# GpSimd's first operation on each weight chunk: a one-source multiply and add in place of the addition of a zero column

## The chip, the cores and the metric

The kernel runs on one core of a Trainium2 chip. The metric is the device time of one launch in microseconds. The notes below call the engines PE (TensorE), DVE (VectorE), ACT (ScalarE), POOL (GpSimd) and SP (SyncE), as the profile does.

## The reference, cut to what matters

A diffusion backbone of four layers takes 512 latent tokens and 128 context tokens (640 columns in all) of width 1024 through one step. Each layer is a token mixer and a dense SwiGLU network:

```
for layer in range(4):
    mixer = (latent attention, bidirectional RWKV-7, multi-scale pooling, latent attention)[layer]
    y = layer_norm(ALPHA * y + gate1 * mixer(modulate(y)))
    y = layer_norm(ALPHA * y + gate2 * swiglu(modulate(y)))      # 1024 -> 2816 -> 1024
```

All arrays are float32. Nearly all of the arithmetic is `h @ W` with a weight matrix that is used once.

## The kernel before

**Split products.** PE multiplies in a rounded float32 type (fp32r). To keep the precision, both factors are split: `hi` is the value rounded to fp32r, `lo` is the value minus `hi`. Each product is the sum of three passes, `w_hi * h_hi + w_lo * h_hi + w_hi * h_lo`. The activations stand as 8 tiles of 128 x 640 (features on partitions, tokens on columns). A matmul takes one 128 x 128 weight tile and 320 columns, so a weight tile costs six matmuls.

**The weight stream.** All weights lie in HBM as 354 chunks of 8 tiles (128 x 1024 elements), in the order of use. SP loads chunk after chunk into `w_raw`, a ring of RAW = 3 slots. POOL turns each into `w_hi` (L680) and `w_lo` (L682) in rings of RS = 4 slots, in the function `split`. POOL may write slot n % 4 once PE has begun with chunk n - 3 (semaphore `w_used`), and PE may read chunk n once `w_split` has counted n + 1. SP loads a new chunk once `w_split` has passed the chunk that stood in its slot. POOL also does small work of the attention heads (`m_diag` L802, `m_hlo` L796) and of the RWKV heads (L712 to L786, among them `s_ys` L763). Its function `stream` walks over the chunks; where 24 chunks or more lie ahead it does so in a hardware loop whose body is 12 chunks, with waits on values that are worked out from the loop's register.

**The activations' side.** At the start of each product stage ACT writes the hi part of each of the 8 tiles, and DVE the lo part as a subtraction of two SBUF tensors: `f_hlo` and `m_hlo` (L2382), in the opening of the RWKV layer `r_hlo` (L2550). There DVE also makes `r_t` (L2566), the token shift with its six mixing weights: 48 tiles of `r_t` and 48 of `r_hlo`. PE's panels (L857, L907) wait for the lo parts tile by tile. In the first attention layer DVE multiplies `x` by a constant (L2279, 8 tiles in place) before the attention output is added to it. In the pooling layer DVE makes the window sums `p_b` (L2854).

**Beside the feed-forward panels.** In layers 0 to 2 DVE also works out the next layer's modulation (`f_acc` L2264, L2262) from SBUF tensors, eight instructions for each of the 22 feature tiles; within one such tile of 128 features PE uses two chunks. DVE also makes `f_a` (L2407) and its lo part `f_alo` (L2409) there.

The order on each engine is that of the code; engines meet only at semaphores.

Of the kernel before, what the change touches and what calls it, by code (L numbers as in the profile page):

```python
# [19 lines left out]
ALU = mybir.AluOpType  # L20
# [3 lines left out]
P = 128  # L24
# [22 lines left out]
CH = 8  # L47
RAW, RS = 3, 4
# [174 lines left out]
def build(nc, a, o):  # L223
    ctx = ExitStack()
    with ctx:
        def sb(name, shape, dt=F32, st=None):
            return (st or ctx).enter_context(nc.sbuf_tensor(name, shape, dt))

        def sem(name):
            return ctx.enter_context(nc.semaphore(name))  # L230
# [4 lines left out]

        x = sb("x", [P, KD, T])
        raw = sb("w_raw", [P, RAW, CH * P])
        zrow = sb("zrow", [P, 1])
        cst = sb("cst", [P, NCST])
        mods = [sb(f"mod{i}", [P, 48, 2]) for i in range(2)]  # L240
        eps = sb("eps", [P, 5])
# [28 lines left out]
        w_hi_done = sem("w_hi_done")  # L270
# [4 lines left out]
        s_init, s_const, s_x = sem("s_init"), sem("s_const"), sem("s_x")  # L275
# [146 lines left out]
        whi = sb("w_hi", [P, RS, CH * P], F32R)  # L422
# [246 lines left out]

        @block.gpsimd  # L670
        def _(pool):
            nc.gpsimd.memset(zrow[:, :], 0.0).then_inc(s_init, 1)
            pool.wait_ge(s_init, 1)

            def split(raw_slot, slot, land, used, n1):
                pool.wait_ge(w_land[raw_slot], land)
                if used is not None:

                    pool.wait_ge(w_used, used)
                nc.gpsimd.tensor_tensor(whi[:, slot, :], raw[:, raw_slot, :], zrow[:, 0:1].to_broadcast([P, CH * P]), ALU.add).then_inc(w_hi_done, 1)  # L680
                pool.wait_ge(w_hi_done, n1)
                nc.gpsimd.tensor_tensor(wlo[:, slot, :], raw[:, raw_slot, :], whi[:, slot, :].bitcast(F32),  # L682
                                        ALU.subtract).then_inc(w_split, 1)

            body = RAW * RS

            def stream(first, last):
                n = first
                while n < last:
                    if n >= body and n % body == 0 and last - n >= 2 * body:  # L690
                        with pool.Fori(n // body, last // body) as i:
                            for u in range(body):
                                split(u % RAW, u % RS, i * (16 * RS) + 16 * (u // RAW + 1), i * body + (u - RS + 1), i * body + (u + 1))
                        n = last // body * body
                    else:
                        split(n % RAW, n % RS, 16 * (n // RAW + 1), n - RS + 1 if n >= RS else None, n + 1)
                        n += 1

            def heads():
                m, q = m_rwb, q_rwb  # L700
# [67 lines left out]
                for i in spans():  # L768
# [11 lines left out]
                    if 0 <= i - 1 < FINAL:  # L780
                        normed(i - 1)
                stream(heads_at, heads_at + 2)
                pool.wait_ge(q.y, 10 * PAIRS)
                pool.wait_ge(q.emptied, FILL["bonus", FINAL])
# [4 lines left out]
            def attention(L):  # L789
                m, q = m_mla[L], q_mla[L]  # L790
                chunk = LAYER_BASE[L] + HEADS_AT + HEADS_AHEAD

                def lo_part(j):
                    for n, (t0, t1) in enumerate(((0, TS), (TS, T))):
                        pool.wait_ge(q.ohi, q.at.ohi + 2 * j + n + 1)
                        nc.gpsimd.tensor_tensor(m.hlo[:, j, t0:t1], m.O[:, t0:t1], m.hhi[:, j, t0:t1].bitcast(F32), ALU.subtract).then_inc(q.olo, 1)  # L796

                def diagonal(j, u):
                    pool.wait_ge(q.rec, q.at.rec + 5 * j + u // 2 + 1)
                    if j:  # L800
                        pool.wait_ge(q.av, q.at.av + 5 * j - (1 if u < 8 else 0))
                    nc.gpsimd.tensor_tensor(m.diag[:, u, :], ident, m.rc[:, u:u + 1].to_broadcast([P, P]), ALU.mult).then_inc(q.diag, 1)  # L802

                for j in range(HEADS // 2):
                    if j:
                        lo_part(j - 1)
                    stream(chunk + j, chunk + j + 1)
                    for u in range(BLOCKS):
                        diagonal(j, u)
                lo_part(HEADS // 2 - 1)  # L810

            mixed = MIXER.index(1)
            heads_at = LAYER_BASE[mixed] + C_RWKV_LORA + C_RWKV_UP + C_RWKV_RKV
            stream(0, HEADS_AT + HEADS_AHEAD)
            attention(0)
            stream(HEADS_AT + HEADS_AHEAD + HEADS // 2, LAYER_BASE[mixed])
            landed, order = [0] * RAW, rwkv_chunks()

            def rwkv_pieces(n0, n1):

                for n, runs in enumerate(order[n0:n1], LAYER_BASE[mixed] + n0):
                    if len(runs) > 1:
                        landed[n % RAW] += 16 * (len(runs) - 1)
                        pool.wait_ge(w_part[n % RAW], landed[n % RAW])
                    split(n % RAW, n % RS, 16 * (n // RAW + 1), n - RS + 1, n + 1)
# [765 lines left out]
        def _(act):  # L1591
# [601 lines left out]


            act.wait_ge(s_const, 16)
            act.wait_ge(s_init, 2)
            ch(af(sc_c[:, :, :], cond, ACT.Silu))
            nc.scalar.copy(sc_hi[:, :, :], sc_c[:, :, :]).then_inc(s_init, 1)
            end()
# [12 lines left out]
        def _(dve):  # L2212
# [682 lines left out]
            nc.vector.memset(eps[:, 2:3], GN_EPS)  # L2895
            nc.vector.memset(eps[:, 3:5], 0.0).then_inc(s_init, 1)
            dve.wait_ge(s_const, 16)
            dve.wait_ge(s_init, 3)
            ch(tt(sc_lo[:, :, :], sc_c[:, :, :], sc_hi[:, :, :].bitcast(F32), ALU.subtract))
            ch(tt(fold, ident[0:4, 0:2], ident[0:4, 2:4], ALU.add))  # L2900
            end()
# [202 lines left out]
```

## Time and profile before

| | us |
|---|---|
| median of 3 runs | 3827.82 |
| lowest and highest of them | 3827.03, 3828.3 |
| span of the profiled execution, first to last instruction | 3817.3 |
| PE busy | 3511.2 |
| DVE busy | 2410.5 |
| POOL busy | 1930.7 |
| ACT busy | 963.8 |

The profiled execution has no time of its own beside its span; the median of the runs stands 10.5 us above that span, which is the work around the first and the last instruction. The busy times overlap: they say how long each engine worked, not what the others waited for.

### The profile page before, as it was taken

Reading aid. Unit: us, or ns where it says so; the run is one execution under the profiler, and the core shown is the slowest. Engines: PE = TensorE matmul, PEld = TensorE weight load, DVE = VectorE, ACT = ScalarE, POOL = GpSimd, SP = SyncE. Lnnn points to the kernel's source line nnn. Section 1 sums busy time; section 2 is a strip of 40 time slices with the busy share of each in tenths; the row PEclk is TensorE's granted clock in tenths of the full one; section 3 lists DMA queues with packets and bytes.
Section 4 is the critical chain, followed back from the end, with each engine's and each line's share of the span. In section 5 each row is a group of like instructions: output and inputs, shape, how many; then the busy total and the mean of one; then the engine's idle time right before and its main releaser. Section 6 shows DMA issues by size and latency. Waiting matters only on the chain.

```text
span 3817.3 us, 74078 instructions
## 1 busy us (share of the span) xinstructions
PE 3511.2 (92%) x31676; PEld 3294.7 (86%) x31676; DVE 2410.5 (63%) x3150; ACT 963.8 (25%) x1950; POOL 1930.7 (51%) x1067
## 2 busy tenths in 40 slices
PE   6899999999789788889999995899999999999998
PEld 2777899999788678888999995799999777899997
DVE  6355688667884467746784769886576555622125
ACT  5433230001243345542300013300012433310010
POOL 1333556665265646626566552466564333566662
PEclk9999999999899889999999997899999999999999
DMA  8200134333145534332343431244332100122221
GB/s 326 62 18 18 45 105 147 129 112 116 67 149 179 147 82 103 87 95 66 123 143 116 127 100 46 90 138 139 112 115 74 31 18 18 56 78 78 73 77 50
DMA packets 226857, 367.67 MB, mean 96 GB/s; under 512 B 104753, under 2 KB 111089, under 8 KB 226417
## 3 DMA queue, kind: packets, MB, share of 16 engines
q1 hardware_dynamic: 171408, 255.08, 22.1%
q10 hardware_dynamic: 55136, 107.98, 8.2%
q8 instruction: 250, 4.10, 0.4%
q14 instruction: 63, 0.51, 0.0%
HBM read 326.47 MB, written 36.54 MB: 95 GB/s over the span
## 4 chain that ended last, share of the span: by engine, by line
PE 77%; DVE 13%; ACT 2%; issue 2%; DMA 2%; SPq 1%; POOL 0%; ACTq 0%; DVEq 0%; POOLq 0%
PE ps L857 58%; PE ps L1118 3%; PE ps L907 2%; PE ps L1131 2%; PE ps L1149 2%; DVE r_t L2566 1%; PE ps L924 1%; DVE x L2362 1%; DVE r_hlo L2550 1%; PE ps L1090 1%; PE ps L1072 1%; DVE x L2371 1%; DVE ps L2715 1%; DVE m_mx L2494 1%; DVE s_T L2714 1%
## 5 line engine op out<-in xcount | busy, mean ns | idle before, releaser
L680 POOL TENSOR_TENSOR w_hi<-w_raw,zrow 128x1024 fp32r<-128x1024 f32 x354 | 695.3, 1964 | 1225.5 <-PE ps L857 879.1
L682 POOL TENSOR_TENSOR w_lo<-w_raw,w_hi 128x1024 fp32r<-128x1024 f32 x354 | 900.3, 2543 | 27.7
L2264 DVE SCALAR_TENSOR_TENSOR f_acc<-f_unit,silu_c,f_acc 128x512 f32<-128x512 f32 x504 | 630.8, 1292 | 7.6
L857 PE MATMUL ps<-f_hhi,w_hi 128*128 128x320 f32 x2688 | 634.2, 317 | 0.0
L857 PE MATMUL ps<-f_hhi,w_lo 128*128 128x320 f32 x2688 | 613.0, 309 | 0.0
L857 PE MATMUL ps<-f_hlo,w_hi 128*128 128x320 f32 x2688 | 610.7, 308 | 0.0
L857 PEld LDWEIGHTS ps<-f_hlo,w_hi 128*128 128x128 f32 x2688 | 449.6, 188 | 0.0
L857 PEld LDWEIGHTS ps<-f_hhi,w_lo 128*128 128x128 f32 x2688 | 449.0, 188 | 0.0
L857 PEld LDWEIGHTS ps<-f_hhi,w_hi 128*128 128x128 f32 x2688 | 441.1, 188 | 0.0
L857 PE MATMUL ps<-f_ahi,w_hi 128*128 128x320 f32 x1408 | 322.0, 310 | 0.0
L857 PE MATMUL ps<-f_alo,w_hi 128*128 128x320 f32 x1408 | 320.8, 309 | 0.0
L857 PE MATMUL ps<-f_ahi,w_lo 128*128 128x320 f32 x1408 | 320.7, 309 | 0.0
L2407 DVE TENSOR_TENSOR f_a<-f_sil,ps 128x640 f32<-128x640 f32 x88 | 72.3, 821 | 373.5 <-ACT f_sil L1677 373.5
L2286 DVE SCALAR_TENSOR_TENSOR x<-ps,mod,x 128x320 f32<-128x320 f32 (+2 forms) x264 | 99.8, 434 | 322.1 <-PE ps L857 320.8
L2409 DVE TENSOR_TENSOR f_alo<-f_a,f_ahi 128x640 fp32r<-128x640 f32 x88 | 202.9, 2306 | 69.9 <-ACT f_ahi L1679 69.9
L1677 ACT ACTIVATE f_sil<-ps 128x640 f32<-128x640 f32 x88 | 62.3, 708 | 711.3 <-DVE f_acc L2264 383.6
L857 PEld LDWEIGHTS ps<-f_ahi,w_hi 128*128 128x128 f32 x1408 | 235.5, 188 | 0.6
L857 PEld LDWEIGHTS ps<-f_ahi,w_lo 128*128 128x128 f32 x1408 | 235.4, 188 | 0.0
L857 PEld LDWEIGHTS ps<-f_alo,w_hi 128*128 128x128 f32 x1408 | 235.3, 188 | 0.0
L1675 ACT COPY mod<-ps 128x8 f32<-128x8 f32 x33 | 5.5, 166 | 652.9 <-PE ps L857 471.9
L1118 PE MATMUL ps<-m_K,m_Q 128*128 128x320 f32 x512 | 162.3, 439 | 8.3 <-DVE m_Q L2480 8.3
L802 POOL TENSOR_TENSOR m_diag<-cst,m_rc 128x128 f32<-128x128 f32 x160 | 60.8, 401 | 208.1 <-DVE m_rc L2507 208.1
(399 smaller groups left out, 6709.9 us busy)
## 6 DMA issues: line engine op xcount, KB each, us to landing
w_raw<-in_w SPq DMA_DIRECT2D x340, 512.0 KB, 3.5
f_unit<-in_ada_w ACTq DMA_DIRECT2D x72, 1024.0 KB, 5.9
ada_ring<-in_ada_w SPq DMA_DIRECT2D x24, 1024.0 KB, 6.6
up_scratch<-r_o ACTq DMA_DIRECT2D x40, 320.0 KB, 2.7
s_LW<-up_scratch SPq DMA_DIRECT2D x16, 320.0 KB, 5.0
s_LA<-up_scratch SPq DMA_DIRECT2D x8, 640.0 KB, 7.1
x<-in_x SPq DMA_DIRECT2D x1, 2560.0 KB, 18.1
x_scratch<-r_o ACTq DMA_DIRECT2D x8, 320.0 KB, 2.2
```

The costliest lines, as they stand in the source:

```text
L680: nc.gpsimd.tensor_tensor(whi[:, slot, :], raw[:, raw_slot, :], zrow[:, 0:1].to_broadcast([P, CH * P]), ALU.add).then_inc(w_hi_done, 1)
L682: nc.gpsimd.tensor_tensor(wlo[:, slot, :], raw[:, raw_slot, :], whi[:, slot, :].bitcast(F32), ALU.subtract).then_inc(w_split, 1)
L857: last = mm(ps[:, 2 * b + h, 0:HT], w, r[:, h * HT:(h + 1) * HT], start=kt == 0 and n < 2, stop=kt == KT - 1 and n >= 4)
L907: last = mm(ps[:, 2 * b + h, 0:HT], w, r[:, h * HT:(h + 1) * HT], start=kt == 0 and n == 0, stop=kt == KT - 1 and n == 2)
L1118: last = mm(ps[:, b + h, 0:HT], query, m.K[:, hh, h * HT:(h + 1) * HT], start=True, stop=True)
L1131: last = nc.tensor.transpose(ps[:, 4 + kb // 4, (kb % 4) * P:(kb % 4 + 1) * P], m.pr[:, u % 2, kb * P:(kb + 1) * P], ident)
L1149: last = mm(ps[HALF[hh], 6, cols], m.V[:, kt, j * P + hh * 64:j * P + hh * 64 + 64], m.pt[:, (5 * j + qt) % 2, hh, n * P:n * P + P], start ...
L1677: af(halves(m.sil[:, f % 2, :]), pair(2 * b), ACT.Silu).then_inc(q.sil, 1)
L2264: last = stt(acc[:, cd, :], unit[:, k, :], by, acc[:, cd, :], ALU.mult, ALU.add)
L2286: last = stt(xs, ps[:, 2 * b + h, t0:t1], gate[:, c, cd:cd + 1], xs, ALU.mult, ALU.add)
L2407: tt(halves(m.a32[:, f % 2, :]), halves(m.sil[:, f % 2, :]), pair(2 * b + 1), ALU.mult).then_inc(q.act, 1)
L2409: tt(m.alo[:, u, :], m.a32[:, f % 2, :], m.ahi[:, u, :].bitcast(F32), ALU.subtract).then_inc(q.lo, 1)
```

## The change

`w_hi` was the sum of the raw chunk and one column of zeros, repeated over the 1024 columns (`to_broadcast`). It becomes a `tensor_scalar`, raw * 1.0 + 0.0, with the constants inside the instruction, so that the raw chunk is the only tensor read. The result is the same rounded value. The column `zrow` (4 bytes in each partition), its memset and one step of the start-up semaphore go. The hardware loop over chunks is replaced by a Python loop, so that each chunk's instructions and constant waits stand in the program by themselves. The subtraction that makes `w_lo` stays as it was.

```diff
-        zrow = sb("zrow", [P, 1])
...
-            nc.gpsimd.memset(zrow[:, :], 0.0).then_inc(s_init, 1)
-            pool.wait_ge(s_init, 1)
-
             def split(raw_slot, slot, land, used, n1):
                 pool.wait_ge(w_land[raw_slot], land)
                 if used is not None:
                     pool.wait_ge(w_used, used)
-                nc.gpsimd.tensor_tensor(whi[:, slot, :], raw[:, raw_slot, :], zrow[:, 0:1].to_broadcast([P, CH * P]), ALU.add).then_inc(w_hi_done, 1)
+                nc.gpsimd.tensor_scalar(whi[:, slot, :], raw[:, raw_slot, :], 1.0, 0.0, ALU.mult, ALU.add).then_inc(w_hi_done, 1)
                 pool.wait_ge(w_hi_done, n1)
                 nc.gpsimd.tensor_tensor(wlo[:, slot, :], raw[:, raw_slot, :], whi[:, slot, :].bitcast(F32),
                                         ALU.subtract).then_inc(w_split, 1)
 
-            body = RAW * RS
-
             def stream(first, last):
-                n = first
-                while n < last:
-                    if n >= body and n % body == 0 and last - n >= 2 * body:
-                        with pool.Fori(n // body, last // body) as i:
-                            for u in range(body):
-                                split(u % RAW, u % RS, i * (16 * RS) + 16 * (u // RAW + 1), i * body + (u - RS + 1), i * body + (u + 1))
-                        n = last // body * body
-                    else:
-                        split(n % RAW, n % RS, 16 * (n // RAW + 1), n - RS + 1 if n >= RS else None, n + 1)
-                        n += 1
+                for n in range(first, last):
+                    split(n % RAW, n % RS, 16 * (n // RAW + 1), n - RS + 1 if n >= RS else None, n + 1)
...
-            act.wait_ge(s_init, 2)
+            act.wait_ge(s_init, 1)
...
-            dve.wait_ge(s_init, 3)
+            dve.wait_ge(s_init, 2)
```

POOL's queue at the head of the program stood so in the kernel before (each row an instruction with its line and what it waits for):

```order
L672 MEMSET zrow 128x1
L680 ISA
L680 TENSOR_TENSOR w_hi<-w_raw,zrow 128x1024 [waits w_land0,s_init]
L682 TENSOR_TENSOR w_lo<-w_raw,w_hi 128x1024 [waits w_hi_done]
L680 TENSOR_TENSOR w_hi<-w_raw,zrow 128x1024 [waits w_land1]
L682 TENSOR_TENSOR w_lo<-w_raw,w_hi 128x1024 [waits w_hi_done]
```

In the changed kernel the same place of POOL's queue reads:

```order
L676 ISA
L676 TENSOR_SCALAR w_hi<-w_raw 128x1024 [waits w_land0]
L678 TENSOR_TENSOR w_lo<-w_raw,w_hi 128x1024 [waits w_hi_done]
L676 TENSOR_SCALAR w_hi<-w_raw 128x1024 [waits w_land1]
L678 TENSOR_TENSOR w_lo<-w_raw,w_hi 128x1024 [waits w_hi_done]
```

The pairs keep their order and their waits; only the kind of the first of each pair is another, and the memset is gone. The end of a loop's body in POOL's queue stood so before, behind the twelfth pair:

```order
L680 TENSOR_TENSOR w_hi<-w_raw,zrow 128x1024 [waits w_used,w_land2]
L681 REGISTER_ALU
L682 TENSOR_TENSOR w_lo<-w_raw,w_hi 128x1024 [waits w_hi_done]
L691 REGISTER_ALU
L691 COMPARE_AND_BRANCH
```

Register arithmetic and the branch go, and the pairs of a loop stand as often as they run. On the other engines no instruction moves.

## Rows read from the trace of the kernel before

**Rows 1.** The page: busy us of each engine, and the chain that ended last.
```profile
PE 3511.2 (92%) x31676; PEld 3294.7 (86%) x31676; DVE 2410.5 (63%) x3150; ACT 963.8 (25%) x1950; POOL 1930.7 (51%) x1067
PE 77%; DVE 13%; ACT 2%; issue 2%; DMA 2%; SPq 1%; POOL 0%; ACTq 0%; DVEq 0%; POOLq 0%
```

**Rows 2.** POOL's groups by form: out, inputs, shape, count, busy us, mean ns.
```profile
L682 POOL TENSOR_TENSOR w_lo<-w_raw,w_hi 128x1024 fp32r<-128x1024 f32 x354 | 900.3, 2543 | 27.7
L680 POOL TENSOR_TENSOR w_hi<-w_raw,zrow 128x1024 fp32r<-128x1024 f32 x354 | 695.3, 1964 | 1225.5 <-PE ps L857 879.1 <-PE ps L907 222.3 <-DMA w_raw<-in_w 77.7
L802 POOL TENSOR_TENSOR m_diag<-cst,m_rc 128x128 f32<-128x128 f32 x160 | 60.8, 401 | 208.1 <-DVE m_rc L2507 208.1
L763 POOL TENSOR_TENSOR s_ys<-s_ys,s_var 128x640 f32<-128x640 f32 x7 | 8.8, 1259 | 9.1 <-DVE s_var L2659 9.1
```

**Rows 3.** Durations of L680 and L682 over the program, ns: least, median, greatest.
```profile
L680 POOL TENSOR_TENSOR w_hi<-w_raw,zrow x354: 1887/1895/2479, 78.5 to 3762.6; 128x1024 fp32r<-128x1024 f32 x177
L682 POOL TENSOR_TENSOR w_lo<-w_raw,w_hi x354: 2340/2412/4316, 80.5 to 3764.6; 128x1024 fp32r<-128x1024 f32 x177
```

**Rows 4.** Timeline of POOL and DVE in the RWKV opening: start, duration, in us.
```profile
1048.60 0.82 DVE L2550 TENSOR_TENSOR r_hlo<-r_t,r_hhi 128x640 fp32r<-128x640 f32 x1
1049.45 0.89 DVE L2566 SCALAR_TENSOR_TENSOR r_t<-r_xx,cst,x 128x640 f32<-128x640 f32 x1
...
1058.35 2.48 POOL L680 TENSOR_TENSOR w_hi<-w_raw,zrow 128x1024 fp32r<-128x1024 f32 x1
1060.90 2.87 POOL L682 TENSOR_TENSOR w_lo<-w_raw,w_hi 128x1024 fp32r<-128x1024 f32 x1
...
1058.99 2.51 DVE L2550 TENSOR_TENSOR r_hlo<-r_t,r_hhi 128x640 fp32r<-128x640 f32 x1
1061.54 2.91 DVE L2566 SCALAR_TENSOR_TENSOR r_t<-r_xx,cst,x 128x640 f32<-128x640 f32 x1
```

**Rows 5.** The chain that ended last, RWKV opening: start, us, what.
```profile
1059.07 2.44 DVE r_hlo L2550
...
1075.17 2.44 DVE r_hlo L2550
...
1101.10 1.23 DVE r_hlo L2550
...
1106.92 2.44 DVE r_hlo L2550
...
1134.58 2.40 DVE r_t L2566
```

**Rows 6.** PE's waits, 1053 to 1163 us: total, times, longest us.
```profile
PE ps L857 <- DVE r_hlo L2550: 15.8, 9, 4.2
```

**Rows 7.** Windows: length, busy of PE, PEld, DVE, ACT, POOL, clock, DMA.
```profile
521.00:960.00 439.00, 439.00 (x3040) 438.68 (x3039) 316.23 (x277) 40.46 (x65) 274.43 (x121) 1.00 0.39 125
...
1073.00:1086.00 13.00, 7.17 (x28) 6.50 (x27) 9.92 (x6) 4.00 (x6) 7.45 (x4) 0.61 0.27 83
```

**Rows 8.** Timeline of DVE and POOL before the first attention layer's output.
```profile
426.24 15.77 DVE L2279 TENSOR_SCALAR x<-x 128x640 f32<-128x640 f32 x8
...
427.51 2.14 POOL L680 TENSOR_TENSOR w_hi<-w_raw,zrow 128x1024 fp32r<-128x1024 f32 x1
```

**Rows 9.** The chain at the start of the first feed-forward stage.
```profile
502.24 1.59 DVE f_hlo L2382
...
505.29 1.46 DVE f_hlo L2382
```

**Rows 10.** Single pieces of the chain: token shift, pooling.
```profile
1020.12 1.23 DVE r_xx L2537
...
2333.39 2.01 DVE p_b L2854
```

**Rows 11.** Idle time of POOL (us, times), and a DVE group, 521 to 900 us.
```profile
  PE ps L857: 135.0, 50
...
L2407 DVE TENSOR_TENSOR f_a<-f_sil,ps 128x640 f32<-128x640 f32 x20 | 16.4, 821 | 51.5 <-ACT f_sil L1677 51.5
```

## The prediction

> **What bounds the kernel now.** I read the page first. PE is busy for 3511.2 of 3817.3 us and makes up 77% of the chain that ended last; DVE makes up 13%, POOL rounds to nothing [rows 1]. So nobody waits for a split chunk as such, and a faster POOL gives PE nothing directly. The feed-forward stretch shows why: over 439 us PE is busy for all 439 at full clock, POOL for 274 [rows 7], and before 50 of its chunks POOL sat idle for 135.0 us until PE gave a slot back, 2.7 us each time [rows 11]. POOL runs three chunks ahead and then waits for PE.
>
> The next view was the timeline of DVE beside POOL, since 13% of the chain is DVE. `r_t` takes 0.89 us and `r_hlo` 0.82 us while POOL is idle. From 1054 us on the same instructions take 2.91 and 2.51 us [rows 4]. The reader is to compare starts and ends: `r_hlo` starts at 1058.99, POOL's L680 started at 1058.35 and ends at 1060.83, and `r_hlo` ends at 1061.50, one usual duration after it. `r_t` then lasts until L682 is over, at 1063.77. So a DVE instruction that reads two SBUF tensors stands still until POOL's running instruction ends, and then does its own work while POOL's next one waits for it: L680 takes 2.48 us here against a median of 1.90, L682 2.87 against 2.41 [rows 3, 4]. The two engines alternate. The Trainium skill says this too (SBUF — State Buffer, "Who interferes with whom"): such a DVE instruction and a reading GpSimd instruction take a shared pair of ports exclusively, for the whole instruction; by that rule, and the trace agrees, the length of POOL's instruction is the price.
>
> What POOL's instructions cost the kernel is therefore what DVE loses behind them in places where PE waits for DVE. The chain shows these places: the openings of stages, where ACT and DVE make the lo parts and POOL, handed its slots back, splits the next chunks at the same moment.
>
> **The price of the new instruction.** The trace has no one-source POOL instruction of any size, so it is bounded. Three groups share the old form, one tensor and one repeated column: 128 columns take 401 ns, 640 take 1259, 1024 take 1895 [rows 2, 3]. Between the first two that is 1.68 ns per column, between the last two 1.66, with 0.19 us for the instruction itself. The full two-tensor form of L682 takes 2.41 us.
> - Low bound: if the time goes by values read and the repeated column counts as a read for each element, one source halves the 1.67 ns: 1024 x 0.835 + 190 = 1.05 us.
> - Middle: going from a full second tensor to a column saved 2.41 - 1.90 = 0.51 us; the same again for dropping the column gives 1.39 us.
> - High bound: nothing excludes a loop that costs as much with one source as with two, or more, since two arithmetic steps replace one. The nearest row for that is L682's, 2.41 us.
>
> I take the low bound, 1.05 us, hence 0.85 us less for each hi, since the two forms in the rows already differ by what their second operand costs. The Trainium skill (GPSIMD Engine Reference, "Elementwise — side-by-side cycle accounting") gives 1.03 cycles per element at 1.2 GHz to a body of one or two operations, as an estimate 0.88 + 0.19 = 1.07 us; that changes the sum by less than half a microsecond.
>
> **The sum.** I went through the chain and took the DVE pieces that end one usual duration after an L680.
> - RWKV opening, 1053 to 1081 us: `r_hlo` takes 2.44 us four times on the chain, the first at 1059.07, the last at 1075.17 [rows 5]. Each waits for most of an L680: 4 x 0.85 = 3.4 us.
> - RWKV opening, 1086 to 1162: three more of that kind, two `r_hlo` of 2.44 (one is shown, at 1106.92) and one `r_t` of 2.40 [rows 5]: 2.6 us. Four `r_hlo` lose only the tail of an L680, the longest taking 1.23 us at 1101.10 [rows 5], 0.4 over its usual 0.82; I count 1.0 for the four. PE waited for `r_hlo` for 15.8 us in the whole stretch [rows 6], so 7.0 us have room.
> - `x` times a constant (L2279): eight instructions take 15.77 us and alternate with three pairs of POOL, each with an L680 of 2.14 us like the first [rows 8]. PE waits for what follows. The ring allows POOL just these three pairs before PE goes on, whatever their speed: 3 x 0.85 = 2.6 us.
> - Five stage starts (near 502, 1821, 2417, 2924 and 3320 us) have an L2382 like the first, which takes 1.59 us and hangs on an L680, and 3 us later one of 1.46, which hangs on the L682 [rows 9]. Such a subtraction takes 0.82 us undisturbed [rows 4], so the L680 costs nearly 0.8 us, and all of that goes; L682 starts earlier too, so the second wait does not grow. 5 x 0.78 = 3.9 us.
> - One piece each in the token shift (`r_xx`, 1.23 us) and the pooling (`p_b`, 2.01 us) [rows 10], and one of the same kind in the opening at 89 us: 3 x 0.85 = 2.6 us.
>
> Together 3.4 + 2.6 + 1.0 + 2.6 + 3.9 + 2.6 = 16.1 us, over some 19 waits for an L680. The granted clock may add to it: in 1073 to 1086 us, after PE's wait of 4.2 us, the mean is 0.61, a part of it at the lower level of 1.2 GHz [rows 6, 7]. Over these 13 us 13 x 0.39 = 5.1 us of full clock are missing, some of them while PE was idle anyway. The wait gets shorter but does not vanish, and I count 0 for the clock, with 4 us as the bound.
>
> **The rest of the change.** The memset and its wait (0.1 us) lie before the first chunk, for which POOL waited 77.7 us [rows 2]: nothing. Register arithmetic and branches run on POOL's sequencer; L680 has no idle time put down to them, and the 2.7 us of slack per chunk cover them [rows 11]: nothing. Without that slack each chunk would cost PE what the sequencer takes. More instructions to fetch: POOL's 926 against 631 rows, beside PE's 31676 matmuls: nothing. A chunk's slot in `w_raw` comes free 0.85 us earlier, so SP issues its load that much earlier, into a queue that nobody waits for.
>
> In the feed-forward stretches the shorter L680 takes waits away from `f_acc` and `f_alo` as well, but there PE is never without work [rows 7], and nothing comes of it.
>
> Against its span of 3817.3 us the profiled execution would come to 3801; the median of the runs lies 10.5 us over that span, so 3827.8 - 16.1 = 3811.7 us.
>
> **The rivals.**
> - *The instruction is hardly faster.* If the loop of GpSimd's program sets the pace and not the number of reads, L680 stays at 1.7 to 1.9 us. For it: the form with one column still costs 1.67 ns per element, three quarters of the full form's 2.17, though a single column hardly needs reading again. Against it: that quarter shows that reading counts. It saves 0 to 0.2 us at 19 places: 3824 to 3828 us. The Trainium skill has such a number as well (same section): 1.8 cycles per element as the best for a tight unrolled loop, as an estimate 1.54 + 0.19 = 1.73 us; by that rule the gain would be 3 us.
> - *The instruction is slower*, because multiply and add are carried out one after the other for each element. Then DVE stands longer behind each of the 19: at L682's 2.41 us it is 19 x 0.51 = 9.7 us, 3837 us; at 2.9 us it is 3847. It decides from 2.3 us on (7.7 us over 19 places). For the feed-forward it needs much more: POOL has 2.7 us free per chunk, and DVE, which had 51.5 us idle before its 20 `f_a` [rows 11], 2.6 us for two chunks; so from about 1.3 us more per L680 on DVE would hold up PE there, once for each of 22 tiles in three layers. Nothing in the trace shows such a program, but nothing shows its opposite.
> - *The gain does not reach PE.* In the RWKV opening ACT's copies and PE's own pace alternate with DVE on the chain, and a DVE that comes out of one wait earlier may run into L682 instead. If half of the 16 us is lost so, it is 3820 us. Against it: at L2279 and the five starts (6.5 us) the chain has nothing but DVE.
>
> **How the numbers follow.** This kernel's measurement can tell 0.2%, 7.7 us, from no change. I give the forecast (L680 at 1.0 to 1.4 us and most of the gain arriving) 0.50, with its own range of 3804 to 3819; half of the gain lost 0.10, mostly still over 7.7 us; hardly faster 0.24; slower 0.16. Faster by over 0.2% is then 0.59, within it 0.25, slower 0.16. The range goes from 3803 (the clock's 4 us, and a little more) to 3830, which leaves out the slower case and little else.
>
> **What the profile of the changed kernel would show.** The price: the median of w_hi's group on POOL, 1.05 us; above 1.7 the forecast is wrong. The lock: `r_hlo` of about 1.6 to 1.7 us where it took 2.51, and L682 and the `r_t` behind it as before. The places: L2279's eight in 13.2 us, PE's wait for `r_hlo` in the RWKV opening some 6 us below 15.8, the L2382 of 1.59 at 0.8. The feed-forward stretches as long as before. If the group shows 1.05 us and the span has not moved, the way from DVE to PE was wrongly read.

## The result and the profile after

| | us |
|---|---|
| changed kernel, median of 4 runs (lowest, highest) | 3797.7 (3793.88, 3803.06) |
| before on the same chip, median of 4 runs | 3827.43 |
| ratio, 95% interval | 0.9923, 0.9909 to 0.9937 |
| span of the profiled execution, and its time | 3792.1, 3793.88 |

The kernel is faster by 29.7 us, 0.77%. 3812 was forecast with a range down to 3803: the direction held, and the time lies below the range. Of all the runs reported here one, of the kernel with `w_lo` in sixteenths, took 4933 us at a mean granted clock of 0.65, where the others had 0.96 to 0.98; ratios leave it out.

First the page's busy line and the chain of the changed kernel:

```profile
PE 3500.5 (92%) x31676; PEld 3284.0 (87%) x31676; DVE 2227.6 (59%) x3150; ACT 963.1 (25%) x1950; POOL 1616.4 (43%) x1066
PE 77%; DVE 12%; ACT 3%; issue 2%; DMA 2%; SPq 1%; POOL 1%; ACTq 0%; DVEq 0%; POOLq 0%
```

Against [rows 1], POOL is busy 314 us less and DVE 183 us less, though no DVE instruction was changed: what left DVE's busy time is standing still. Next POOL's two groups by form (as [rows 2]), and the least, median and greatest durations (as [rows 3]):

```profile
L678 POOL TENSOR_TENSOR w_lo<-w_raw,w_hi 128x1024 fp32r<-128x1024 f32 x354 | 883.1, 2495 | 29.6
L676 POOL TENSOR_SCALAR w_hi<-w_raw 128x1024 fp32r<-128x1024 f32 x354 | 398.4, 1126 | 1495.7 <-PE ps L843 1136.0 <-PE ps L893 227.2 <-DMA w_raw<-in_w 78.0
...
L676 POOL TENSOR_SCALAR w_hi<-w_raw x354: 1037/1047/2190, 78.4 to 3737.4; 128x1024 fp32r<-128x1024 f32 x177
L678 POOL TENSOR_TENSOR w_lo<-w_raw,w_hi x354: 2340/2412/4306, 79.6 to 3738.5; 128x1024 fp32r<-128x1024 f32 x177
```

`w_hi`'s median is 1047 ns, the 1.05 us of the forecast; `w_lo` is unchanged. Now the timeline of POOL, then of DVE, in the RWKV opening, the place of [rows 4], and last a pair of POOL and DVE from its end:

```profile
1048.41 1.63 POOL L676 TENSOR_SCALAR w_hi<-w_raw 128x1024 fp32r<-128x1024 f32 x1
1050.13 2.86 POOL L678 TENSOR_TENSOR w_lo<-w_raw,w_hi 128x1024 fp32r<-128x1024 f32 x1
...
1049.17 1.54 DVE L2552 SCALAR_TENSOR_TENSOR r_t<-r_xx,cst,x 128x640 f32<-128x640 f32 x1
1050.64 3.03 DVE L2536 TENSOR_TENSOR r_hlo<-r_t,r_hhi 128x640 fp32r<-128x640 f32 x1
...
1164.91 1.35 POOL L676 TENSOR_SCALAR w_hi<-w_raw 128x1024 fp32r<-128x1024 f32 x1 [3.33 <-PE ps L843]
...
1165.28 1.66 DVE L2536 TENSOR_TENSOR r_hlo<-r_t,r_hhi 128x640 fp32r<-128x640 f32 x1
```

The two engines still alternate, but they have changed partners: `r_t` now stands behind `w_hi`, `r_hlo` behind `w_lo`. `r_t` takes 1.54 us against 0.89 undisturbed, so it is held for 0.65 us. Before, `r_hlo` took 2.51 against 0.82 behind the old `w_hi`, held for 1.69 us [rows 4]. These two numbers can't be subtracted: they are two different DVE instructions, and each now meets the other one of POOL's. What can be compared is a whole turn of the two engines. `r_hlo` and `r_t` together took 2.51 + 2.91 = 5.42 us beside one pair of POOL [rows 4], and take 1.54 + 3.03 = 4.57 us now: 0.85 us less, just what `w_hi` became shorter. The one `r_hlo` that does meet a `w_hi` from its start, at 1165.28, takes 1.66 us where it took 2.51, again 0.85 less. It ends at 1166.94, POOL's instruction at 1166.26.

The other named places: PE's waits in 1040 to 1148 us (as [rows 6]); DVE's and POOL's timeline at the first attention layer's output (as [rows 8]); and the chain at the first feed-forward stage's start (as [rows 9]):

```profile
PE ps L843 <- DVE r_hlo L2536: 8.9, 7, 2.7
```
```profile
422.80 13.26 DVE L2265 TENSOR_SCALAR x<-x 128x640 f32<-128x640 f32 x8
...
424.08 1.28 POOL L676 TENSOR_SCALAR w_hi<-w_raw 128x1024 fp32r<-128x1024 f32 x1
```
```profile
494.73 0.74 DVE f_hlo L2368
...
496.94 1.46 DVE f_hlo L2368
```

PE waits for `r_hlo` for 8.9 us in place of 15.8, the eight instructions take 13.26 us (13.2 was forecast), and the first `f_hlo` (0.74 us on the chain) is undisturbed while the second (1.46) still stands behind `w_lo`. Last, windows of the changed kernel (columns as [rows 7]): its feed-forward stretch, and the 10 us after PE's wait for L2265's successor. Under them the same 10 us of the kernel before:

```profile
513.00:952.00 439.00, 439.00 (x3039) 438.68 (x3039) 275.02 (x277) 40.17 (x65) 220.44 (x121) 1.00 0.39 125
437.00:447.00 10.00, 9.71 (x63) 9.40 (x64) 4.78 (x11) 1.52 (x3) 4.48 (x3) 1.00 0.30 102
```
```profile
443.00:453.00 10.00, 9.77 (x52) 9.24 (x53) 3.50 (x7) 1.47 (x2) 4.31 (x2) 0.83 0.29 100
```

In its 439 us of the feed-forward PE is busy throughout, as before. In the 10 us behind the wait the granted clock was 0.83 before, a part of it at the lower level of 1.2 GHz, and is 1.00 now. PE's wait ahead of it fell from 3.3 to 0.8 us.

**Where the gain lies.** Each PE matmul of one profile can be set against the same one of another. The table gives how many us earlier than in the first profile of before PE starts it, at eight times of that profile; each number is a difference of two start times. The kernels that the argument rests on are in it.

| kernel | 150 | 500 | 960 | 1050 | 1163 | 1230 | 1760 | 3780 |
|---|---|---|---|---|---|---|---|---|
| before, again | -2.6 | -3.6 | -3.8 | -3.8 | -3.9 | -3.9 | -10.6 | -10.8 |
| only the loop | 0.1 | 0.2 | -0.1 | 0.0 | -0.1 | -0.2 | -6.8 | -7.2 |
| changed | 3.4 | 7.5 | 8.1 | 8.7 | 16.1 | 17.0 | 18.3 | 25.2 |
| changed, again | 3.3 | 7.4 | 8.1 | 8.7 | 16.3 | 17.2 | 8.6 | 14.5 |
| with memset | 0.5 | 0.4 | 0.3 | 0.6 | 9.1 | 9.8 | 10.4 | 10.4 |
| `w_hi` twice | 1.2 | 6.3 | 6.2 | 6.3 | 6.7 | 6.6 | 3.6 | 2.8 |
| one step | 3.3 | 8.5 | 8.3 | 8.9 | 18.0 | 18.4 | 15.5 | 15.1 |
| `w_lo` in 8 | 6.4 | 11.4 | 14.0 | 16.3 | 30.6 | 31.2 | 28.6 | 38.8 |
| `w_lo` in 16 | 6.6 | 11.7 | 14.7 | 17.3 | 23.6 | 23.0 | 17.0 | 26.8 |

Changed and changed again agree within 0.2 us up to 1230 us, and stand 9.7 us apart at 1760, behind the RWKV heads; before and its copies part by 6.6 us there. This stretch, in which PE waits for small work on all engines, has a length of its own in each execution. The windows below cut the same 529 us out of the two profiles of the changed kernel, the first and the repeated one:

```profile
1213.00:1742.00 529.00, 442.54 (x10932) 407.24 (x10932) 319.76 (x731) 244.18 (x678) 281.87 (x182) 0.93 0.39 101
```
```profile
1213.00:1742.00 529.00, 441.26 (x10862) 406.06 (x10862) 319.48 (x725) 243.72 (x676) 272.74 (x177) 0.91 0.39 99
```

The repeated one has the lower mean granted clock, 0.91 against 0.93, and starts 70 matmuls fewer in it. Outside the heads the change is worth 17.0 + (25.2 - 18.3) = 23.9 us in one profile and 17.2 + 5.9 = 23.1 in the other. So against the first profile of before some 23 to 24 us are the change's. That profile is one draw too: its copy loses 4.1 us to it outside the heads, 2.6 of them in the first 150 us, and against the copy the change would be worth 27 to 28 us. That what the first medians show beyond 24 us (29.7 in all, 24.2 in the repeated runs) is such spread is argued from these profiles, not shown.

### The profile page after: what moved, and what is told of

Read it like the earlier page. It is cut to its first block, busy times and chain, and to the rows that moved or that the text cites. A ratio compares the mean times of both kernels' runs of the same rounds, so it can differ in the third digit from the quotient of the medians.

```text
span 3792.1 us, 73712 instructions
## 1 busy us (share of the span) xinstructions
PE 3500.5 (92%) x31676; PEld 3284.0 (87%) x31676; DVE 2227.6 (59%) x3150; ACT 963.1 (25%) x1950; POOL 1616.4 (43%) x1066
## 4 chain that ended last, share of the span: by engine, by line
PE 77%; DVE 12%; ACT 3%; issue 2%; DMA 2%; SPq 1%; POOL 1%; ACTq 0%; DVEq 0%; POOLq 0%
PE ps L843 59%; PE ps L1104 3%; PE ps L893 2%; PE ps L1117 2%; PE ps L1135 2%; DVE x L2348 1%; PE ps L910 1%; DVE r_hlo L2536 1%; PE ps L1076 1%; DVE x L2357 1%; PE ps L1058 1%; DVE ps L2701 1%; DVE m_mx L2480 1%; DVE s_T L2700 1%; DMA inv_scratch<-s_L 1%
## 5 line engine op out<-in xcount | busy, mean ns | idle before, releaser
L676 POOL TENSOR_SCALAR w_hi<-w_raw 128x1024 fp32r<-128x1024 f32 x354 | 398.4, 1126 | 1495.7 <-PE ps L843 1136.0
L678 POOL TENSOR_TENSOR w_lo<-w_raw,w_hi 128x1024 fp32r<-128x1024 f32 x354 | 883.1, 2495 | 29.6
L2250 DVE SCALAR_TENSOR_TENSOR f_acc<-f_unit,silu_c,f_acc 128x512 f32<-128x512 f32 x504 | 551.1, 1134 | 7.6
L2395 DVE TENSOR_TENSOR f_alo<-f_a,f_ahi 128x640 fp32r<-128x640 f32 x88 | 173.4, 1970 | 69.9 <-ACT f_ahi L1665 69.9
L1744 ACT ACTIVATE m_P<-ps,m_neg 128x640 f32<-128x640 f32 (+1 forms) x160 | 113.4, 709 | 166.0 <-DVE m_neg L2481 165.9
```

The source lines that it names most:

```text
L676: nc.gpsimd.tensor_scalar(whi[:, slot, :], raw[:, raw_slot, :], 1.0, 0.0, ALU.mult, ALU.add).then_inc(w_hi_done, 1)
L1744: af(dst, s, ACT.Exp, bias=m.neg[:, u % 2:u % 2 + 1], scale=SM_SCALE, accum_out=m.total[:, u:u + 1]).then_inc(q.pexp, 1)
L2250: last = stt(acc[:, cd, :], unit[:, k, :], by, acc[:, cd, :], ALU.mult, ALU.add)
L2395: tt(m.alo[:, u, :], m.a32[:, f % 2, :], m.ahi[:, u, :].bitcast(F32), ALU.subtract).then_inc(q.lo, 1)
```

## The experiments

All were timed beside the kernel before on their own chip. None leaves out a part of the computation; some do a part twice or write a tile once more than needed. Short diffs are against the changed kernel, where nothing else is said.

**The same kernel again.** No edit.

> The changed kernel as it is, to get more runs of it with their spans and granted clocks. Its four runs so far took 3793.9 to 3803.1 us at a mean granted clock of 0.972 to 0.967. If the spread is one of the clock, the runs line up: the lower the mean clock of a run, the longer it is, about 1.8 us for 0.001. If the spread has another cause, time and clock do not go together. Expected median 3798 us.

3799.21 us (6 runs, 3784.79 to 3804.56) against 3823.41 (27 runs), ratio 0.9932 (0.9916 to 0.9949): 24.2 us faster. Over its six runs the time falls as the mean clock rises, from 3804.56 us at 0.968 to 3784.79 at 0.973, with one run out of line (3802.66 at 0.967). That time and clock go together does not say which makes the other: a kernel whose PE waits longer is granted less clock behind the wait, as the 10 us above show.

**Only the loop.** The kernel before, with `stream` written out and the zero column kept.

```diff
-                n = first
-                while n < last:
...
+                for n in range(first, last):
+                    split(n % RAW, n % RS, 16 * (n // RAW + 1), n - RS + 1 if n >= RS else None, n + 1)
```

> The kernel before with its loop over chunks written out, the addition of the zero column kept. My theory: the loop is worth nothing, since POOL waits 2.7 us per chunk for PE; 3825 to 3829 us. Rival: the register arithmetic between the pair's halves and the branch delay POOL in the stage openings, and part of the 30 us comes from the loop; then 3815 to 3822 us.

3822.1 us (12 runs), ratio 0.9996 (0.9985 to 1.0007). The table has it within 0.2 us of before at each mark up to 1230. So the loop by itself is worth nothing, and the gain is put down to the new form of `w_hi`. The arithmetic with the hardware loop kept wasn't tried.

**A write without a read in front.**

```diff
+                nc.gpsimd.memset(wlo[:, slot, :].bitcast(F32), 0.0).then_inc(w_hi_done, 1)
+                pool.wait_ge(w_hi_done, 2 * n1 - 1)
                 nc.gpsimd.tensor_scalar(whi[:, slot, :], raw[:, raw_slot, :], 1.0, 0.0, ALU.mult, ALU.add).then_inc(w_hi_done, 1)
-                pool.wait_ge(w_hi_done, n1)
+                pool.wait_ge(w_hi_done, 2 * n1)
```

> The changed kernel with a memset of the chunk's w_lo slot ahead of each w_hi, so that POOL is busy longer for each chunk (how long, its group will show; between 0.5 and 1.2 us) with an instruction that reads nothing. If DVE is held up only by POOL instructions that read SBUF, the time stays near the changed kernel's, at 3797 to 3803 us. Rival: it is POOL's being busy or late that counts, whatever it does; then each memset costs as much at the 19 to 25 places as the change saved, and the time goes back to 3815 to 3828 us.

3809.29 us (10 runs), ratio 0.9965 (0.9953 to 0.9976). The time lies between the two expectations. With the memset (955 ns in the mean) POOL works about as long for each chunk as before, and still 8.5 us are gained in the RWKV opening (0.6 to 9.1 in the table), where DVE reads two tensors. At the first attention layer's output, where DVE's instruction has one source, nothing is gained, and neither is it at the stage starts (10.4 at 1760 and at 3780). The timeline of this kernel, first at the attention output, then twice in the RWKV opening, POOL's rows ahead of DVE's:

```profile
427.02 0.95 POOL L676 MEMSET w_lo<- 128x1024 f32 x1
...
425.76 15.85 DVE L2267 TENSOR_SCALAR x<-x 128x640 f32<-128x640 f32 x8
...
1053.97 1.05 POOL L678 TENSOR_SCALAR w_hi<-w_raw 128x1024 fp32r<-128x1024 f32 x1
...
1054.55 1.14 DVE L2538 TENSOR_TENSOR r_hlo<-r_t,r_hhi 128x640 fp32r<-128x640 f32 x1 [1.50 <-ACT r_hhi L1782]
...
1057.90 0.95 POOL L676 MEMSET w_lo<- 128x1024 f32 x1
...
1058.56 0.81 DVE L2538 TENSOR_TENSOR r_hlo<-r_t,r_hhi 128x640 fp32r<-128x640 f32 x1
```

The eight take 15.85 us, as with the long `w_hi` (15.77 in [rows 8]). The `r_hlo` at 1058.56 starts inside a memset and takes 0.81 us, its undisturbed time, while the one at 1054.55 is held for 0.3 us by the rest of a `w_hi`. So what counts is the kind of access, not how long POOL is busy. At the stage starts the meeting point takes the gain back: the first `f_hlo`, at 501.77, is free, but `w_hi` and with it `w_lo` come later by the memset, and the next `f_hlo` meets nearly all of `w_lo` and takes 2.64 us in place of 1.52 in the changed kernel. The Trainium skill (SBUF — State Buffer, "Who interferes with whom") says the same: a VectorE instruction with two SBUF inputs contends with a GpSimd instruction that reads SBUF and not with one that only writes it, while `tensor_scalar` in a two-port mode contends with both. The rows at 1058.56 and at 425.76 agree; that the eight ran in such a mode no row says.

**`w_hi` made twice.**

```diff
+                nc.gpsimd.tensor_scalar(whi[:, slot, :], raw[:, raw_slot, :], 1.0, 0.0, ALU.mult, ALU.add).then_inc(w_hi_done, 1)
+                pool.wait_ge(w_hi_done, 2 * n1 - 1)
                 nc.gpsimd.tensor_scalar(whi[:, slot, :], raw[:, raw_slot, :], 1.0, 0.0, ALU.mult, ALU.add).then_inc(w_hi_done, 1)
-                pool.wait_ge(w_hi_done, n1)
+                pool.wait_ge(w_hi_done, 2 * n1)
```

> The changed kernel with each w_hi made twice, one after the other, so that POOL reads for 2.1 us again in place of 1.05, in two instructions. Theory of the lock: DVE waits out one instruction and then runs between the two, so where DVE has work ready it pays 1.05 us twice instead of 1.9 once; the time goes back to 3820 to 3835 us. Rival (POOL's reads do not matter, the gain came from elsewhere): it stays at 3797 to 3803 us.

3812.53 us (12 runs), ratio 0.9976 (0.9968 to 0.9985), between the two expectations. The gain in the RWKV opening shrinks from 7.5 to 0.4 us, that at the attention output stays (1.2 to 6.3 in the table). In the opening two short reads cost DVE as much as the one long one. At the attention output the eight take 11.89 us, less than the changed kernel's 13.26: two pieces of `w_lo` fall into them, where three do in the changed kernel.

**Before again.** No edit of the kernel before.

> The kernel before as it is, for a second profile and spans beside its times. My prediction took the 10.5 us between the first profile's span and the median of the timed runs for work outside the span. Theory: outside the span there are only about 2 us, and the first profile was a quick draw; then this run's span is within 3 us of its time, and the difference between the profiles lies in the stretch of the RWKV heads (530 us long at first). Rival: the profiled execution is of another kind than the timed ones, and its span is again some 10 us below the median.

3819.96 us (10 runs, 3809.92 to 3831.28), ratio 0.9995 (0.9983 to 1.0007). The profiled span is 3828.1 us and its time 3829.93. In every profile here that has a time on record, the time lies 1.7 to 1.9 us above the span.

**`w_lo` in pieces: halves, quarters, eighths, sixteenths.** The same edit with 2, 4, 8 and 16:

```diff
-                nc.gpsimd.tensor_tensor(wlo[:, slot, :], raw[:, raw_slot, :], whi[:, slot, :].bitcast(F32),
-                                        ALU.subtract).then_inc(w_split, 1)
+                q4 = CH * P // 8
+                for c0 in range(0, 8 * q4, q4):
+                    last = nc.gpsimd.tensor_tensor(wlo[:, slot, c0:c0 + q4], raw[:, raw_slot, c0:c0 + q4],
+                                                   whi[:, slot, c0:c0 + q4].bitcast(F32), ALU.subtract)
+                last.then_inc(w_split, 1)
```

> The changed kernel with each w_lo made in two halves of 512 columns, about 1.25 us each in place of 2.41. Theory of the lock by instruction: DVE gets in between the halves, so where it stood 2.4 us behind a w_lo it stands 1.25; of the 36 us that the chain still loses behind w_lo some 8 to 15 come back: 3784 to 3791 us. Rival: what counts is the sum of POOL's reading, which grows by the fixed cost of a second instruction (0.19 us); then the time is 3797 to 3803 us.

> As the halves, but w_lo in four pieces of 256 columns, about 0.7 us each, 2.9 us together. Theory of the lock by instruction: a little better than the halves where DVE has work queued (DVE stands 0.7 us a piece), 3780 to 3790 us. Rival: POOL, which now yields to DVE four times for each chunk, comes late with the chunks after a stage opening and PE waits for w_lo; then it is above the halves, 3790 to 3805 us.

> The changed kernel with each w_lo in eight pieces of 128 columns, about 0.4 us each, 3.2 us together. Quarters took 3785.6 us, halves 3790.6, the whole 3797.7 to 3799.2. If shorter turns at the port go on paying, 3780 to 3785 us; if POOL's growing sum (4.3 us for each chunk with w_hi) takes it back where DVE and POOL alternate, 3786 to 3792 us. I expect the second, near 3786.

> The changed kernel with w_lo made in sixteen pieces of 64 columns. The pieces of 128 columns took a median of 462 ns and their mean was 566 ns, the eight together some 3.7 to 4.5 us for each chunk. By the fall from 741 ns (256 columns) to 462 ns (128) a piece of 64 should take 0.29 to 0.36 us, sixteen of them 4.7 to 5.8 us, and with w_hi's 1.05 us GpSimd needs 5.8 to 6.9 us for each chunk, where TensorE needs 7.1 us for the chunk's matmuls. Theory: a VectorE instruction is held for what is left of GpSimd's running read, so the stretches with stalls still gain a little (up to 3 us), but GpSimd's slack is nearly gone and TensorE begins to wait for w_lo in the stretches where both stream: 3777 to 3800 us. Rival: the slack is enough and the gain goes on: below 3777 us.

| | us (runs) | ratio, 95% interval | median piece, ns |
|---|---|---|---|
| whole | 3797.7 (4) | 0.9923, 0.9909 to 0.9937 | 2412 |
| halves | 3790.6 (5) | 0.9921, 0.9906 to 0.9935 | 1296, 1322 |
| quarters | 3785.58 (5) | 0.9902, 0.9887 to 0.9916 | 741 |
| eighths | 3777.35 (4) | 0.9874, 0.9853 to 0.9895 | 462 |
| sixteenths | 3791.86 (3) | 0.9911, 0.989 to 0.9933 | 322 |

The ratios of whole and halves can't be told apart, and neighbours' intervals overlap; whole and eighths are clearly apart. Outside the heads the gain on the first profile of before is 24, 26, 34, 42 and 32 us in this order. Up to eighths, more work on POOL makes the kernel faster. That was not foreseen for the eighths: 3786 us was expected. POOL's groups of the eighths:

```profile
L680 POOL TENSOR_TENSOR w_lo<-w_raw,w_hi 128x128 fp32r<-128x128 f32 x2832 | 1501.9, 566 | 29.6
L676 POOL TENSOR_SCALAR w_hi<-w_raw 128x1024 fp32r<-128x1024 f32 x354 | 396.5, 1120 | 882.1 <-PE ps L846 561.9 <-PE ps L896 198.3 <-DMA w_raw<-in_w 77.7
```

and of the sixteenths, with PE's waits between 1030 and 1148 us under them:

```profile
L680 POOL TENSOR_TENSOR w_lo<-w_raw,w_hi 128x64 fp32r<-128x64 f32 x5664 | 1975.1, 387 | 29.6
L676 POOL TENSOR_SCALAR w_hi<-w_raw 128x1024 fp32r<-128x1024 f32 x354 | 383.8, 1084 | 463.4 <-PE ps L896 179.5 <-PE ps L846 177.0 <-DMA w_raw<-in_w 77.7
```
```profile
PE ps L846 <- POOL w_lo L680: 8.8, 6, 2.2
PE ps L846 <- DVE r_hlo L2539: 3.0, 3, 1.8
```

The pieces make `w_lo` 883 us of POOL's time, then 1502, then 1975, while its idle time before `w_hi` falls from 1496 to 882 and 463 us. With eighths PE waits for POOL's `w_lo` nowhere in the program. With sixteenths it waits for `w_lo` for 8.8 us in the RWKV opening, where POOL cannot run ahead, and for 11.6 us in all. There the gain turns; in the table the sixteenths lead by 1.0 us at 1050 and trail by 7.0 at 1163. Eighths make the fastest kernel of this study, 1.26% below before.

**One arithmetic step.**

```diff
-                nc.gpsimd.tensor_scalar(whi[:, slot, :], raw[:, raw_slot, :], 1.0, 0.0, ALU.mult, ALU.add).then_inc(w_hi_done, 1)
+                nc.gpsimd.tensor_scalar(whi[:, slot, :], raw[:, raw_slot, :], 1.0, None, ALU.mult).then_inc(w_hi_done, 1)
```

> The changed kernel with w_hi as raw * 1.0 alone, one arithmetic step in place of two. If the port sets the pace, w_hi's group stays at a median of 1.05 us and the time within 2 us of the changed kernel's. If the steps set it, the group falls below 1.0 us and the time falls with it by 20 times the difference.

3805.07 us (5 runs), ratio 0.996 (0.9947 to 0.9973). Neither expectation came true, and this run decides the mechanism, because the instruction came out long. Durations of this kernel's `w_hi`, then POOL's and DVE's timeline twice in the RWKV opening, then both at the first attention layer's output and at the first feed-forward stage's start:

```profile
L676 POOL TENSOR_SCALAR w_hi<-w_raw x354: 2767/2774/3356, 79.3 to 3747.5; 128x1024 fp32r<-128x1024 f32 x177
```
```profile
1050.26 3.35 POOL L676 TENSOR_SCALAR w_hi<-w_raw 128x1024 fp32r<-128x1024 f32 x1
1053.70 2.79 POOL L678 TENSOR_TENSOR w_lo<-w_raw,w_hi 128x1024 fp32r<-128x1024 f32 x1
...
1051.02 1.54 DVE L2552 SCALAR_TENSOR_TENSOR r_t<-r_xx,cst,x 128x640 f32<-128x640 f32 x1
1052.48 0.81 DVE L2536 TENSOR_TENSOR r_hlo<-r_t,r_hhi 128x640 fp32r<-128x640 f32 x1
...
1074.48 3.35 POOL L676 TENSOR_SCALAR w_hi<-w_raw 128x1024 fp32r<-128x1024 f32 x1
...
1075.12 1.65 DVE L2536 TENSOR_TENSOR r_hlo<-r_t,r_hhi 128x640 fp32r<-128x640 f32 x1
...
424.20 3.32 POOL L676 TENSOR_SCALAR w_hi<-w_raw 128x1024 fp32r<-128x1024 f32 x1
...
422.92 8.80 DVE L2265 TENSOR_SCALAR x<-x 128x640 f32<-128x640 f32 x8
...
492.82 2.78 POOL L676 TENSOR_SCALAR w_hi<-w_raw 128x1024 fp32r<-128x1024 f32 x1 [14.35 <-PE ps L893]
495.69 2.34 POOL L678 TENSOR_TENSOR w_lo<-w_raw,w_hi 128x1024 fp32r<-128x1024 f32 x1
...
493.71 0.83 DVE L2368 TENSOR_TENSOR f_hlo<-f_t,f_hhi 128x640 fp32r<-128x640 f32 x1
...
495.93 2.78 DVE L2368 TENSOR_TENSOR f_hlo<-f_t,f_hhi 128x640 fp32r<-128x640 f32 x1
```

`w_hi` takes 2.77 us, 0.88 more than the zero-column form, yet the kernel is 0.4% faster than before. `r_t` is held for the same 0.65 us as behind the 1.05 us form, and the next `r_hlo` runs undisturbed inside the same `w_hi`, which goes on until 1053.61. An `r_hlo` that meets a `w_hi` from its start, at 1075.12, takes 1.65 us, as the 1.66 beside the 1.05 us form, though POOL's instruction goes on for 1.06 us behind it. So this form lets DVE go long before its end. The `f_hlo` at 493.71 starts 0.89 us after a `w_hi` that nothing delayed and is free (0.83 us); before, the `f_hlo` at the same distance was held and took 1.59 us on the chain [rows 9]. By an estimate from the pair at 1074 the hold lasts until about 1.0 us into the form's undisturbed run: `r_hlo` starts 0.64 us after `w_hi` and is held for 0.83, together 1.47. Off go the 0.58 us by which `w_hi` itself was delayed there (3.35 against 2.77). On come 0.14 us, by which a held `r_hlo` of the other forms ends sooner than POOL's end and its own 0.82 us would give. The eight instructions at the attention output take 8.80 us in place of 13.26, beside a `w_hi` of 3.32; one `w_lo` falls into them in place of three. What the long form does cost is phase: `f_hlo` at 493.71 is free, but `w_lo` then starts at 495.69 and the next `f_hlo` meets all of it, 2.78 us in place of 1.52. In the table it keeps pace with the changed kernel to 1230 us and gains nothing at later stage starts.

**Halves of `w_hi` beside quarters of `w_lo`.** Against the quarters:

```diff
-                nc.gpsimd.tensor_scalar(whi[:, slot, :], raw[:, raw_slot, :], 1.0, 0.0, ALU.mult, ALU.add).then_inc(w_hi_done, 1)
+                h2 = CH * P // 2
+                nc.gpsimd.tensor_scalar(whi[:, slot, 0:h2], raw[:, raw_slot, 0:h2], 1.0, 0.0, ALU.mult, ALU.add)
+                nc.gpsimd.tensor_scalar(whi[:, slot, h2:], raw[:, raw_slot, h2:], 1.0, 0.0, ALU.mult, ALU.add).then_inc(w_hi_done, 1)
```

> The quarters with w_hi in two halves as well. The trace of the changed kernel shows DVE standing 0.65 us behind a w_hi of 1.05 us and also 0.65 us behind the one-step w_hi of 2.77 us, so behind half of it it should stand 0.33 us. Gain where DVE is blocked by w_hi: some 10 places at 0.3 us, 3 us at most, less the second instruction's 0.19 us; 3782 to 3787 us. Rival: no difference at all from the quarters' 3785.6.

3788.8 us (4 runs), ratio 0.9911 (0.9888 to 0.9933): not to be told from the quarters alone (0.9902), the rival of the expectation. A half takes 622 ns in the median, 1.24 us for two in place of 1.05. By this run there is little left to win behind `w_hi`.

**The zero column kept, `w_lo` in quarters.** The kernel before with the edit of the quarters.

> The kernel before (zero column added, hardware loop) with w_lo in quarters. It tells whether the two gains add up: the form of w_hi gave 24 to 30 us, the quarters another 12 to 14 us on top. If each is the time that DVE stands behind its own instruction, the quarters alone give 10 to 15 us: 3808 to 3813 us. Rival: with the long w_hi kept, DVE only moves from one wait into the other, and the quarters give less than 5 us: 3818 to 3823 us.

3803.41 us (5 runs), ratio 0.9942 (0.9922 to 0.9962). Cutting `w_lo` alone brings 22 us without the change, more than the 10 to 15 expected; the two together bring about 38 (0.9902), less than 22 and the change's 24 to 30, so they take partly the same waits.

## Why the prediction was off

**Right.** The bound, and that POOL matters only through the time DVE stands: DVE's busy time fell with POOL's. The price of the instruction (1047 ns against 1.05 us), and 0.85 us less for DVE at each `w_hi` it stands behind (5.42 to 4.57 us a turn, and 2.51 to 1.66 for `r_hlo`). The loop, memset and fetch at nothing (0.9996 for the loop alone). The feed-forward at nothing (the same matching of matmuls gives 8.1 us at 521 and at 960). L2279's eight: 13.26 us against 13.2, worth 2.5 us of PE's time. The RWKV opening: 7.5 us against 7.0, with PE's wait for `r_hlo` 6.9 us shorter against "some 6". The first `f_hlo` of a stage start at 0.74 us on the chain against 0.8.

**The step that failed is the sum.** Its 16.1 us were 23.9 in the first profile, because three of its terms were too small: the opening at 89 us, the clock at nothing, and the stage starts. They follow below. Even so the time would have stood in the range: 3827.8 - 23.9 = 3803.9 us, against a lower end of 3803. The last 6 us, which put the median at 3797.7, lie within what runs of one kernel differ by (3784.79 to 3804.56 for the changed one, medians of before from 3822.91 to 3827.43 in the groups here). So that it fell outside the range is partly a matter of the draw; that the sum was a third too low is not.

**Right here, but too wide: "the length of POOL's instruction is the price".** For the zero-column form and the new one it holds: an `r_hlo` met from its start takes 2.51 us beside one and 1.66 beside the other, the 0.85 us between their lengths. It is no rule for every instruction of POOL: beside the 2.77 us form the same `r_hlo` takes 1.65, and beside a memset 0.81. A reading that fits all four is that DVE's two-tensor instructions are held while GpSimd reads, and that the long form is done reading early; no run measures the reads. That the rule carried over to the new form was luck: for a one-source form of 2.77 us the prediction has its "slower" rival, and the one-step kernel is 0.4% faster than before. The sign "`r_hlo` of about 1.6 to 1.7 us where it took 2.51" came true at 1165.28 only; in most of the opening `r_hlo` met `w_lo` and took 3.03 us, since a shorter `w_hi` changes which DVE instruction meets which of POOL's.

**Mis-sized: "one of the same kind in the opening at 89 us", 0.85 us.** It was 3.4. The chain has four small DVE pieces there, each ending with one of POOL's instructions, two with a `w_hi` and two with a `w_lo` that a `w_hi` stands ahead of. Chain of before, then of the changed kernel (the fourth, `lna`, ends with a `w_lo` and takes 2.19 us in both):

```profile
87.77 1.46 DVE mod L2231
...
89.25 1.76 DVE mod L2234
...
93.43 1.88 DVE hmod L2239 x2
```
```profile
86.87 0.62 DVE mod L2217
...
87.52 0.91 DVE mod L2220
...
90.85 1.02 DVE hmod L2225 x2
```

The three shrink by 0.84, 0.85 and 0.86 us, and the chain reaches the first of them 0.9 us earlier. That is four times the 0.85 us of one `w_hi`. These small instructions (16 or 96 columns) have little work of their own; they last until POOL's end, and I had taken one row where the whole string had to be counted. Here before and its copy differ by 2.6 us (the table at 150), so this term is known less well than the others.

**Mis-sized: "I count 0 for the clock".** After L2279 the stretch with a lower clock is gone, and PE gains 1.6 us more after 443 us than the shorter wait itself gave; 17% of 10 us at full clock are 1.7 us. The memset kernel, whose wait there stayed (3.4 us), does not gain it; every kernel whose wait shrank does. Behind the RWKV opening it is another 0.9 us (16.1 to 17.0): from there to 1230 PE is busy without a gap in both kernels, for 67 us at a mean granted clock of 0.97 before and for 66 at 0.98. Together 2.5 us, inside the bound of 4.

**Mis-sized: five stage starts at 3.9 us.** They gave 0.6, 0.9, 2.3, 1.3 and 0.8 us, together 6.0, and 0.8, 1.6, 0.5, 1.8 and 0.9 in the repeated profile, together 5.6. The first `f_hlo` of each gave some 0.8 us, as counted; what is beyond it comes from the instructions behind it, and falls otherwise in each execution. The pooling's piece gave 1.6 (1.1 when repeated) and `r_xx` 0.5, together 2.1 against the 1.7 counted.

Against the 16.1 us that makes, with the first profile: opening +2.6, clock +2.5, stage starts +2.1, RWKV opening +0.5, single pieces +0.4, L2279 -0.1, in all 24.1, against the 23.9 read from the table.

**Wrong: "the median of the runs lies 10.5 us over that span".** A profiled time lies 1.7 to 1.9 us over its span. Most of the rest was a quick draw of the heads in the profile: the two later profiles with the old `w_hi` need 6.6 and 6.7 us more there. Nothing was lost by it in the difference, but it means that a single profile's span is no anchor within 0.3%, and the three first runs (3827.03 to 3828.3) hid how far runs of one kernel spread (3809.92 to 3831.28).

**The rivals.** "Hardly faster" and "slower" fell with the 1047 ns (the one-step run shows that a slow form was there to be had). "The gain does not reach PE" fell too: 23.9 us arrived, more than was counted. I had given it 0.10 and nothing to the opposite, that more reaches PE than was counted; the clock and the small instructions are that case.

What stays open is how the single-step form reads and writes its data, and why the long form releases DVE as early as the short one; no run here measures GpSimd's reads by themselves. That the heads' spread is the chip's own and not started by something earlier in the kernel is argued from identical kernels that differ there, not shown.

## What to carry to other kernels

When an engine off the critical path shares something with one that is on it, ask not how long its instructions are but how long each keeps the other standing, and measure that as the other's duration beside it less its undisturbed duration. Shorter instructions can pay without less work: cutting `w_lo` into eighths cost GpSimd 600 us and gained another 0.5%, and with sixteenths the slack was used up and TensorE waited. Compare like with like: one instruction beside its old and its new neighbour, or a whole turn of the two engines, since a change of one length changes who meets whom. And count every small instruction on the chain: one that ends together with another engine's is nearly all wait.

## What the runs showed of the hardware

- On GpSimd a `tensor_scalar` with two arithmetic steps over 128x1024 (float32 to fp32r) takes 1047 ns, the same with one step 2774 ns. I had expected the single step to be no slower. The Trainium skill (GPSIMD Engine Reference, "Elementwise — side-by-side cycle accounting") gives one figure, 1.03 cycles per element, to bodies of up to two operations. The two-step row agrees with it, the one-step row does not, and the measurement decides.
- A VectorE subtraction of two SBUF tensors (128x640) that meets the whole of GpSimd's instruction takes 2.51 us beside the form with a repeated column (1895 ns), 1.66 beside the two-step form (1047 ns) and 1.65 beside the one-step form (2774 ns), against 0.82 undisturbed. Beside a GpSimd memset it takes 0.81. The Trainium skill (SBUF — State Buffer, "Who interferes with whom") calls the port pair that the two engines share an exclusive lock, and says of VectorE's two-port modes that whoever issues first has it for the whole instruction. The first two forms show that for two SBUF inputs as well; the 2774 ns form does not, and the measurement decides.
- A GpSimd subtraction of two tensors takes 2412 ns for 1024 columns, 741 for 256, 462 for 128 and 322 for 64.
